# LRU gate matmuls of a two-block model as 64x64 quarters of the array, with a half-swapped copy of the convolved tile

## What is computed

```python
def rglru(u, w_a, b_a, w_x, b_x, lam, reverse):       # u is the convolved input, (1, 512, 512)
    uh = uf.reshape(bsz, s, LRU_HEADS, LRU_HEAD_DIM)  # 8 heads of 64 channels
    r = sigmoid(einsum('bshi,hij->bshj', uh, w_a) + b_a)
    i = sigmoid(einsum('bshi,hij->bshj', uh, w_x) + b_x)
    log_a = LRU_C * r * log_sigmoid(lam)
    a = exp(log_a)
    bterm = sqrt(-expm1(2.0 * log_a)) * (i * uf)
    h = scan(a, bterm, reverse)                       # h[t] = a[t] * h[t-1] + bterm[t]

c = centred_depthwise_conv(lru_x, conv_w, conv_b)
h_f = rglru(c, lru_wa_f, lru_ba_f, lru_wx_f, lru_bx_f, lru_lam_f, reverse=False)
h_b = rglru(c, lru_wa_b, lru_ba_b, lru_wx_b, lru_bx_b, lru_lam_b, reverse=True)
y_lru = gelu(lru_gate) * (h_f + h_b)
```

## Time and profile before

| | |
|---|---|
| time, median of 3 runs (lowest to highest) | 1522.42 us (1521.64 to 1522.47) |
| the profiled execution | 1521.82 us, of which the span from the first to the last instruction is 1520.0 us |
| mean granted TensorE clock, as a share of 2.4 GHz | 0.989 |
| busy: PE, DVE, ACT, POOL | 1388.6, 563.9, 315.7, 129.5 us |

### The profile page before, as it was taken

How to read it: one execution, slowest core, us unless ns; L and a number is a source line. 1 busy time by engine, 2 the same in 40 slices (tenths; PEclk the granted TensorE clock), 3 DMA queues, 4 the chain that set the end, 5 groups by cost and what they waited for, 6 DMA issues and landing times.

```text
span 1520.0 us, 16865 instructions
## 1 busy us (share of the span) xinstructions
PE 1388.6 (91%) x6743; PEld 759.7 (50%) x6743; DVE 563.9 (37%) x979; ACT 315.7 (21%) x501; POOL 129.5 (9%) x203
## 2 busy tenths in 40 slices
PE   7999699999988988988988989989879999999997
PEld 5878333433332332333323323323368877888875
DVE  6785611211111101201201201201189588846663
ACT  6582200110010000000100100100153254424322
POOL 1030000000000000000000000000022314441001
PEclk9999899999999999999999999999989999999999
DMA  9025589999999999999999999999936222244231
GB/s 333 1 92 241 221 366 427 428 426 428 428 428 429 429 429 428 429 428 429 428 428 429 429 428 429 428 429 428 408 106 179 69 73 80 81 152 169 86 108 56
DMA packets 67469, 465.19 MB, mean 306 GB/s; under 512 B 5472, under 2 KB 32352, under 8 KB 42720
## 3 DMA queue, kind: packets, MB, share of 16 engines
q1 hardware_dynamic: 63152, 454.71, 72.5%
q0 software_dynamic: 3984, 9.41, 2.4%
q10 hardware_dynamic: 288, 0.45, 0.1%
HBM read 457.76 MB, written 6.78 MB: 306 GB/s over the span
## 4 chain that ended last, share of the span: by engine, by line
PE 56%; DMA 35%; DVE 5%; ACT 2%; issue 1%; SPq 0%; POOL 0%; DVEq 0%; POOLq 0%; ACTq 0%
DMA wide<-in_w_down 23%; PE bank L819 14%; DMA early<-in_w_down 11%; PE bank L614 8%; PE bank L616 8%; PE bank L615 8%; PE bank L846 6%; PE bank L859 4%; PE bank L783 1%; PE bank L790 1%; ACT ring_r L1055 1%; DMA ring<-in_w_in 1%; PE bank L903 1%; PE bank L929 1%; DVE ring_r L1457 1%
## 5 line engine op out<-in xcount | busy, mean ns | idle before, releaser
L819 PE MATMUL bank<-wide,xinT 128*64 128x512 f32 x1376 | 306.8, 596 | 47.7 <-DMA wide<-in_w_up 26.8
L819 PEld LDWEIGHTS bank<-wide,xinT 128*64 128x64 f32 x1376 | 95.6, 137 | 257.2 <-issue 171.8
L1460 DVE SCALAR_TENSOR_TENSOR th<-th,bank 128x512 f32<-128x512 f32 x32 | 20.6, 684 | 431.7 <-ACT th L1190 431.7
L819 PE MATMUL bank<-early,xinT 128*64 128x512 f32 x672 | 150.5, 596 | 25.5 <-DMA early<-in_w_up 15.2
L846 PE MATMUL bank<-wide,actT 128*64 128x512 f32 x688 | 153.0, 594 | 3.8 <-issue 3.0
L614 PE MATMUL bank<-hT_lo,ring_r 128*128 128x512 f32 x352 | 139.9, 397 | 0.3 <-ACT st L1039 0.3
L616 PE MATMUL bank<-hT_hi,ring_r 128*128 128x512 f32 x352 | 137.1, 390 | 0.0
L615 PE MATMUL bank<-hT_hi,ring_r 128*128 128x512 f32 x352 | 137.0, 389 | 0.0
L1190 ACT ACTIVATE th<-bank 128x512 f32<-128x512 f32 x32 | 17.4, 594 | 515.1 <-PE bank L819 515.1
L819 PEld LDWEIGHTS bank<-early,xinT 128*64 128x64 f32 x672 | 46.0, 137 | 129.1 <-issue 79.0
L1457 DVE TENSOR_TENSOR ring_r<-ring,ring_r 128x2048 fp32r<-128x2048 f32 x38 | 88.2, 2321 | 48.9 <-ACT ring_r L1055 48.6
(11 more groups left out here) (355 smaller groups left out, 1685.3 us busy)
## 6 DMA issues: line engine op xcount, KB each, us to landing
wide<-in_w_gate SPq DMA_DIRECT2D x43, 2048.0 KB, 40.1
wide<-in_w_up SPq DMA_DIRECT2D x43, 2048.0 KB, 39.1
wide<-in_w_down SPq DMA_DIRECT2D x43, 2048.0 KB, 38.4
early<-in_w_gate SPq DMA_DIRECT2D x21, 2048.0 KB, 40.2
early<-in_w_up SPq DMA_DIRECT2D x21, 2048.0 KB, 39.2
early<-in_w_down SPq DMA_DIRECT2D x21, 2048.0 KB, 38.5
ring<-in_w_in SPq DMA_DIRECT2D x26, 1024.0 KB, 5.5
ring<-in_w_out SPq DMA_DIRECT2D x8, 1024.0 KB, 5.0
```

Of the source, the lines that this page charges most:

```text
L819: last = pe.matmul(bank[1 + 2 * (m % 2) + q // 2][o:o + 64, :], xinT[:, k, :], w[:, i, q * 512:(q + 1) * 512], start=(k == 0), stop=(k == ...
L1460: return dve.scalar_tensor_tensor(out_, a, s, b, op0, op1)
```

## The change

The two gates of a direction are computed with 64x64 blocks. Of the first gate of a direction (index 2d) the block of head a lies where it was, on the diagonal, and multiplies `conv`. Of the second gate (index 2d + 1) the two blocks now lie off the diagonal in `wbd`: the weights of head a take the 64 rows of the other half. So its input must stand in the other half as well: `swapped` is a new SBUF tile of 128x512 with the upper and the lower 64 partitions of `conv[:, c, :]` exchanged. GpSimd makes it with two DMAs per tile from SBUF to SBUF, 64 partitions of 2 KB each, that is 128 KB. There is one such buffer. The copy for tile c waits for `conv_ready` and, from the second tile on, for the last matmul of lru{c-1}. TensorE waits for both DMAs of the tile (`swap_in`) at the head of the group. A group is then eight fp32 matmuls 64x64 by 64x512 instead of four of 128x128, and a gate's semaphore is raised with the last of its two. The copies of tiles 0 to 2 stand ahead of all gelu work on GpSimd, that of tile 3 between the gelu arguments of tiles 0 and 1.

```diff
+        swapped = area("swapped", max(ends["fold"], ends["sin_part"]), S)
...
+        swap_in = sem("swap_in")
...
                     pe.wait_ge(conv_ready, n + 1)
-                    for i in range(4):
-                        b = start(f"lru{n}_{i}")
-                        finish(f"lru{n}_{i}", pe.matmul(b[:, :], wbd[:, 4 * i + n, :], conv[:, n, :], start=True, stop=True))
+                    pe.wait_ge(swap_in, 32 * (n + 1))
+                    for d in range(2):
+                        one, two = start(f"lru{n}_{2 * d}"), start(f"lru{n}_{2 * d + 1}")
+                        for a in range(2):
+                            here, there = slice(64 * a, 64 * a + 64), slice(64 - 64 * a, 128 - 64 * a)
+                            first = pe.matmul(one[here, :], wbd[here, 8 * d + n, here], conv[here, n, :],
+                                              start=True, stop=True)
+                            second = pe.matmul(two[here, :], wbd[there, 8 * d + 4 + n, here], swapped[there, :],
+                                               start=True, stop=True)
+                        finish(f"lru{n}_{2 * d}", first)
+                        finish(f"lru{n}_{2 * d + 1}", second)
...
             roots(0, 0)
+
+            def swap(c):
+
+                pool.wait_ge(conv_ready, c + 1)
+                if c:
+                    full(pool, f"lru{c - 1}_3")
+                for a in range(2):
+                    pool.dma_start(swapped[64 - 64 * a:128 - 64 * a, :], conv[64 * a:64 * a + 64, c, :]).then_inc(swap_in, 16)
+
+            for c in range(CT - 1):
+                swap(c)
             for c in range(CT):
 
+                if c == 1:
+                    swap(CT - 1)
                 was_read(pool, f"in{8 + c}")
...
         for a in range(2):
-            bd[64 * a:64 * a + 64, j, :, 64 * a:64 * a + 64] = w[:, a].transpose(1, 0, 2)
+            at = 64 * ((a + j) % 2)
+            bd[at:at + 64, j, :, 64 * a:64 * a + 64] = w[:, a].transpose(1, 0, 2)
```

## The result

| | before | after |
|---|---|---|
| median of 20 runs each (lowest to highest) | 1521.78 us (1520.28 to 1524.48) | 1526.02 us (1523.62 to 1528.0) |
| ratio | | 1.0027, 95% interval 1.0021 to 1.0034 |
| profiled execution: span, mean granted clock | 1520.0 us, 0.989 | 1524.1 us, 0.987 |

The changed kernel is slower by 4.2 us, 0.27%. The median of 1526.02 lies inside the range (1520.0 to 1526.6) but above the forecast of 1523.1 and above the forecast's own range, which ended at 1525.3. The text gave "slower by over 0.2%" a chance of 0.23.

The account below looks back on a forecast made before the run. The prediction took the weight stream to bound the experts, and TensorE's path through lru0 and lru1 to set their start. Stall 2.3, matmuls -2.4, clock +0.8 gave +0.7 on 1522.42: 1523.1 us, range 1520.0 to 1526.6.

Parts of the forecast that it names:

- the forecast's own range: Whole kernel: 1521.4 to 1525.3 us, from stalls of 1.4 to 3.6 us and a clock loss of 0 to 1.7.
- slower by over 0.2%: Whole kernel above 1525.5 us: the two slow cases and a little of the forecast's upper end; chance 0.23.
- The copy for tile 0: Ahead of lru0: second half issued at 29.7 us, lands 5.2 us later at 34.9, stalling TensorE 2.3 us.
- the loaded lines: Earlier GpSimd DMA landings beside weight loads, 4.3 to 6.5 us, giving tile 0's copy a stall of 1.4 to 3.6.
- later than every loaded row of its size: Rival for tile 0's copy: landing takes 9 us, stall 6.1, total 1527.8 us; chance 0.08.
- The matmuls: lru groups on TensorE: four quarters at once, 2.2 us a group, saving 1.2 each, 2.4 for lru0 and lru1.
- The changes of shape: On entering and leaving each lru group: 0.5 us for the two changes, counted within the group's 2.2.
- The clock: TensorE's clock may fall after the stall ahead of lru0: bounds 0 and 1.7 us, half taken, +0.8.
- The fall is there already, so I count nothing new: Ahead of the mixing products at 109 to 111 us: idle time grows to some 4.5 us, no added clock loss.
- two at a time: Rival at the lru groups: row halves sharing a PSUM bank run in pairs, 3.9 us a group, 1526.5 total; chance 0.13.
- copies 1 to 3 cost nothing: Ahead of lru1 to lru3: these copies land before they are needed, even at 6.5 us; cost nothing.
- the recurrence hid the delay of `gates(0)`: On VectorE: gates(0) begins 2.5 us later, but idle times of 1.36 and 1.79 us absorb it.

Follow-up runs that it names:

- e6: Changed kernel plus six unused fp32 matmuls of 512 columns on TensorE ahead of the wait for tile 0's copy; 1524.59 us.
- e4: Changed kernel with the four 128x128 matmuls per group of the kernel before, keeping the copies and TensorE's waits, though nothing reads the copy; 1527.26 us.
- e2: Changed kernel with the loads of dft_s and the first two units of w_out issued only after tile 0's copy has landed; 1520.08 us.
- e10: Changed kernel with only the two w_out loads held until tile 0's copy has landed, dft_s still queued ahead; 1520.17 us.
- e9: Kernel before plus two unused fp32 matmuls of 448 columns in TensorE's idle time ahead of the first output product; 1520.26 us.

## Why the prediction was right or wrong, point by point

**The copy for tile 0: wrong in size, and this is the step that failed.** The prediction took 5.2 us to landing, between the loaded lines of the earlier trace rows, a stall of 2.3 with 3.6 as its upper bound. It was 7.2 us from 30.41, a stall of 5.05, in the profile of the changed kernel, and 6.1 and 6.2 us in those of e6 and e4, whose loads and copies are the same. Its argument was that the engines are full from 28 to 36 us, which is right, and that the loaded rows are the nearest, which they are. But it read how busy the engines were and not how much was queued on them: SyncE had issued the 645 KB of `dft_s` at 21.2 us and the 2 MB of `w_out` from 24.2 on, and at 30.4, when the second copy was issued, none of the three had landed. For the second copy e2, e10 and the changed kernel give 2.5, 3.5 and 7.2 us with none, one and three of these loads issued ahead of it. The trace of before had the landings of these loads (32.81, 35.37 and 37.86); seen afterwards, the copy landed at 36.4 to 37.6 with all three queued, between the last two, where the upper bound from the durations of other DMAs was 36.2. A second part of the miss is the issue: the second copy went out at 30.41 in place of 29.7, 0.7 of the 2.75 us, since GpSimd began 0.3 us behind the end of the convolution and its first issue took 0.745 us in place of 0.53.

**The rival "later than every loaded row of its size"** comes nearest: priced with 9 us and a stall of 6.1 at 1527.8, given 0.08. Its direction was right and its chance much too low; it gave no cause, and its 9 us are more than any landing measured.

**The matmuls: right, a little cautious.** Four at once, with steps of 0.43 us; 1.99 us a group where 2.2 was taken, a saving of 1.45 in place of 1.2. The changes of shape cost 0.27 us a group in sum (1.99 - 4 x 0.429), not 0.5: that was the mis-sized term. On the path the two groups should have given 2.9 us; 1.4 of it went with the clock.

**The clock: right that it can fall, low in size.** +0.8 was taken, with 1.7 as bound; 1.4 us was lost behind a wait of 4.89 us, longer than the 2.3 that was priced. e6 shows the clock's share apart from the wait.

**"The fall is there already, so I count nothing new" was wrong.** Behind the longer idle time ahead of the mixing products 0.55 us more was lost in these two profiles. And the fall is not always there already: e4 had none behind 2.16 us. Of before's executions in the first two sets, 22 ran at a mean clock of 0.990, with 1520.36 to 1521.43 us, and 30 at 0.987 to 0.989, with 1521.58 to 1522.91. That the lower group is the one without this fall fits e4, e9 and the sizes, but no profile of such an execution of before was taken, so it stays an inference. In the third set only 3 of 19 were in the lower group.

**The sum.** The terms as measured are 0.17 + 5.05 - 2.9 + 1.4 = 3.7 us at the mixing products (3.68 in the profile), and with the 0.55 behind them 4.2 (4.23 at the first expert). Against the +0.7 of the forecast the stall was 2.75 us larger, the late start adds 0.17, the clock 0.6 at lru0 and 0.55 at 111 us, and the matmuls give 0.5 back: 3.6 in sum. The stall alone would have taken the forecast past 1525.5, the bound of "slower by over 0.2%". That the median still lies inside the outer range is luck: its upper end, 1526.6, was set by the rival of quarters two at a time (1526.5), which the trace refutes, and the forecast's own range ended 0.7 below what was measured.

**The rival "two at a time" is refuted.** The row halves of one gate write one bank, on partitions 0 to 63 and 64 to 127, and all four quarters start together (52.21 to 52.23). The Trainium skill quotes the vendor that different row tiles can't access one bank at the same time (PSUM — Partial Sum Buffer, PSUM bank collisions raise a hardware error). Here they do, and at no cost in time; the same section's own measurement concerns row tiles that write the same 32 partitions of a bank, which no run here does.

**What held:** copies 1 to 3 cost nothing in the changed kernel (landed 44.78, 57.79 and 86.20, needed 52.21, 80.58 and 93.57); the recurrence hid the delay of `gates(0)` (VectorE's idle time at the fold went from 1.79 us to 0.38, still waiting for ScalarE); GpSimd had the time for eight issues; the experts followed the first one (4.23 us at 190, 4.1 in the span). The forecast that the first expert would come within 1 us of 190.28 failed with the stall.

## What to carry to other kernels

Price a DMA that is added to the path by what is queued on the DMA engines when it is issued, with the landings of the loads that are outstanding at that moment as a bound, and not by the duration of other DMAs of its size (one kind of copy under one set of loads shows this here, at three depths); if it must be early, hold back the loads that nobody needs yet, or let an engine with nothing to do make the copy (64 partitions to the other 64 in 1.29 us on ScalarE). An idle time of TensorE on the path can cost twice, once as itself and once by the clock behind it (it did behind 3.93 to 4.89 us, not behind e10's 1.21 at lru0 nor e4's 2.16), and time saved ahead of a wait elsewhere makes that idle time longer; a few unused matmuls in it gave 1.4 to 2 us, but in e6 they also outlasted the wait by about 1.5. Where the profile names a releaser for an instruction with several semaphores, look whether that one had long been done.

## What the runs showed of the hardware that was not expected

- Four 64x64 quarters run at once with the two row halves in one PSUM bank on separate partitions: 16 fp32 passes of 512 columns in 1.72 us and 0.27 for the changes of shape. The rows start in fours of L739, L741, L739, L741, so the first passes of all four quarters seem to run ahead of the second ones.
- An idle time of TensorE of 2.17 us (before) was followed by a clock of 0.50 and one of 2.16 us (e4) was not. Around idle times of 3.93 to 4.89 us, ahead of lru0 and of the mixing products, it fell in every profile taken, though not for the same time.
- A copy of 128 KB within SBUF takes 2.1 to 2.5 us with none of these loads queued ahead, 2.9 and 3.5 with 645 KB, and 5.7 to 7.2 with 2.6 MB, whether GpSimd or ScalarE issues it.
